# A hybrid decoder step on one core: all sample key products in the prompt search, value gathers behind them

## What is computed

```python
def trunk_layer(x, conv_past, ffn_past, attend, p):
    xn = rms_norm(x, g_attn)
    a_in, q, k, v, qi, ki, wi, ga, gb = split_in(xn @ w_in)
    glu = a_in[..., :D_CONV] * jax.nn.sigmoid(a_in[..., D_CONV:])
    h = layer_norm(causal_dwconv(glu_ext, conv_w, conv_b), ln_g, ln_b)
    y_a = jax.nn.silu(h) @ w_a_out
    q = rms_norm(q.reshape(b, t, N_HEADS, HEAD_DIM), q_g)
    k = rms_norm(k.reshape(b, t, N_HEADS, HEAD_DIM), k_g)
    o = attend(q, k, v, qi, ki, wi)
    x = x + (jax.nn.sigmoid(ga) * y_a + jax.nn.sigmoid(gb) * (o.reshape(b, t, D_ATTN) @ w_b_out)) @ w_o
...

def attend(q, k, v, qi, ki, wi):        # prompt and samples alike
    score = jnp.einsum('bqhl,bqh->bql', relu(qi . ki), wi) * IDX_SCALE   # future positions -inf
    idx = lax.top_k(score, n_keep)[1]
    logits = jnp.einsum('bqhd,bqkhd->bqhk', q, k_sel) * ATTN_SCALE + rel_bias[rel_bucket(q_pos - key_pos)]
    p = jax.nn.softmax(jnp.where(rel >= 0, logits, -inf))
    return jnp.einsum('bqhk,bqkhd->bqhd', p, v_sel)
```

## Time and profile before

| | |
|---|---|
| median of 3 runs | 1239.48 us (1238.52 to 1245.93) |
| the profiled execution | 1239.93 us |
| its span | 1238.1 us |
| busy: PE, DVE, ACT, POOL | 90%, 64%, 25%, 14% of the span |
| prompt search, steps 3 to 32 | 379 to 502 us |
| first head of the attention | 541.59 us |
| attention | 541.59 to 723.29 us |
| from yb to the end | 723.29 to 1238 us |
| mean granted clock of TensorE | 0.945 of 2.4 GHz |

### The profile page before, as it was taken

How to read it: one execution, slowest core, us unless ns; L and a number is a source line. 1 busy time by engine, 2 the same in 40 slices (tenths; PEclk the granted TensorE clock), 3 DMA queues, 4 the chain that set the end, 5 groups by cost and what they waited for, 6 DMA issues and landing times.

```text
span 1238.1 us, 16818 instructions
## 1 busy us (share of the span) xinstructions
PE 1111.8 (90%) x6732; PEld 894.5 (72%) x6732; DVE 788.8 (64%) x1576; ACT 311.1 (25%) x633; POOL 177.4 (14%) x187
## 2 busy tenths in 40 slices
PE   5999799999779998977574789999999999989996
PEld 3668688664557743435343368999999999989996
DVE  5299999688779889867571144586666565642211
ACT  2111233222201134422121223432223221241220
POOL 0011110000011123153673400000000000001011
PEclk9999899999889999986786899999999999999998
DMA  9110550013143455244765533123332323123230
GB/s 306 44 68 7 179 180 1 31 38 137 69 168 120 144 170 170 80 147 121 220 212 187 174 92 103 35 69 86 86 97 75 103 69 103 48 77 112 81 112 28
DMA packets 109607, 134.49 MB, mean 109 GB/s; under 512 B 8081, under 2 KB 76588, under 8 KB 108484
## 3 DMA queue, kind: packets, MB, share of 16 engines
q1 hardware_dynamic: 90997, 76.67, 20.4%
q0 software_dynamic: 13184, 45.42, 11.7%
q10 hardware_dynamic: 5349, 11.34, 2.6%
HBM read 127.89 MB, written 5.51 MB: 108 GB/s over the span
## 4 chain that ended last, share of the span: by engine, by line
PE 70%; DVE 18%; ACT 4%; issue 3%; another core or an unknown queue 3%; DMA 0%; ACTq 0%; DVEq 0%
PE G L1265 12%; PE G L1267 12%; PE G L1266 12%; PE G L990 8%; PE G L755 6%; PE G L775 6%; DVE hT L1482 4%; PE TB L1112 2%; ACT late L2240 2%; DVE junk L1576 2%; PE UB L1208 1%; DVE ksel L1792 1%; PE G L1081 1%; DVE scoreT L1544 1%
## 5 line engine op out<-in xcount | busy, mean ns | idle before, releaser
L1265 PE MATMUL G<-xnH,whi 128*128 128x274 f32 x704 | 205.2, 291 | 1.1 <-DVE aext L1947 0.7
L1266 PE MATMUL G<-xnL,whi 128*128 128x274 f32 x704 | 203.5, 289 | 0.0
L1267 PE MATMUL G<-xnH,wlo 128*128 128x274 f32 x704 | 202.9, 288 | 0.0
L990 PE MATMUL G<-xnT,wring 128*128 128x280 f32 x512 | 141.4, 431 | 9.0 <-ACT sgb L2036 3.7
L1878 DVE TENSOR_TENSOR wlo<-wraw,whi 128x2048 fp32r<-128x2048 f32 (+1 forms) x38 | 76.4, 2011 | 91.1 <-ACT whi L2400 90.3
L1265 PEld LDWEIGHTS G<-xnH,whi 128*128 128x128 f32 x704 | 132.4, 188 | 1.7 <-issue 0.9
L1266 PEld LDWEIGHTS G<-xnL,whi 128*128 128x128 f32 x704 | 133.3, 189 | 0.0
L1267 PEld LDWEIGHTS G<-xnH,wlo 128*128 128x128 f32 x704 | 133.1, 189 | 0.0
L990 PEld LDWEIGHTS G<-xnT,wring 128*128 128x128 f32 x512 | 100.7, 203 | 39.9 <-issue 7.1
L2540 POOL DMA_INDIRECT ksel<-in_cache_k_dram,gather_row x64 | 70.5, 1102 | 351.6 <-DVE gather_row L1744 180.1
L1265 PE MATMUL G<-hfH,whi 128*128 128x274 f32 x352 | 102.6, 292 | 0.0
(11 more groups left out here) (417 smaller groups left out, 1970.5 us busy)
## 6 DMA issues: line engine op xcount, KB each, us to landing
wraw<-in_w_up_dram SPq DMA_DIRECT2D x44, 512.0 KB, 5.1
wring<-in_w_in_dram SPq DMA_DIRECT2D x8, 2048.0 KB
wraw<-in_w_down_dram SPq DMA_DIRECT2D x16, 704.0 KB, 4.4
qB<-scr_q SPq DMA_DIRECT2D x32, 256.0 KB
wring<-in_w_in_dram ACTq DMA_DIRECT2D x3, 2048.0 KB
wring<-in_w_o_dram SPq DMA_DIRECT2D x2, 2048.0 KB
toep<-scr_toep SPq DMA_DIRECT2D x1, 2432.0 KB, 15.4
wqi<-in_w_in_dram SPq DMA_DIRECT2D x2, 1024.0 KB, 9.8
```

Source lines behind the costliest of these rows:

```text
L990: last = pe.matmul(out[:, i, 0:b - a], w[:, j, c:c + P], x[:, j, a:b], start=(j == 0), stop=(j == depth - 1))
L1265: pe.matmul(out, w_hi, x_hi, start=start, stop=False)
L1266: pe.matmul(out, w_hi, x_lo, start=False, stop=False)
L1267: return pe.matmul(out, w_lo, x_hi, start=False, stop=stop)
```

## The change

The kernel after differs in where things stand in the engines' lists, and in the buffers of the values.

- DVE: all 32 key products stand in the search, one a step from step 3 and two in steps 16 and 24. Before, 14 stood there at every second step, 2 between the masks and 16 in the heads. The takes of ya are at steps 7 to 12. The norms of row tiles 1, 2, 3 stand in steps 27, 29, 31, `first_max` in step 28, and all three masks behind the search. Steps 9 and 10 are counted by ACT too.
- The norm of the last tile and the sample attention's pieces come at earlier heads.
- TensorE: the first `tokens` come ahead of head 8's transposes.
- ACT: the counts stand at other places of its list; from step 28 on, takes, copies, squares and the first tile's exponentials stand between them.
- POOL: all keys, then v's rows, then all values, into twelve buffers. SP's list is unchanged.

```diff
-    TOKENS_AT = {11: 0, 13: 1}
+    TOKENS_AT = {9: 0, 11: 1}
...
-    AT_BIAS, AT_LOGITS = {12: 0, 29: 1}, {13: 0, 29: 1}
-    AT_MAX, AT_WEIGHTS, AT_PROBS, AT_OUT = {14: 0, 30: 1}, {15: 0, 31: 1}, {16: 0, 32: 1}, {28: 0, 39: 1}
-    AT_QUADS = {17: 0, 19: 1, 22: 2, 27: 3, 33: 4, 35: 5, 37: 6, 39: 7}
-    FIRST_KEYS = 14
-    AT_KEYS = {11: 16, 13: 17, 14: 18, 15: 19, 16: 20, 17: 21, 18: 22, **{a: a + 3 for a in range(20, 29)}}
-    AT_LAST_ROW, AT_LAST_MASK = 11, 19
-    FIRST_TAKE = 9
+    AT_BIAS, AT_LOGITS = {11: 0, 22: 1}, {12: 0, 23: 1}
+    AT_MAX, AT_WEIGHTS, AT_PROBS, AT_OUT = {13: 0, 24: 1}, {14: 0, 25: 1}, {15: 0, 26: 1}, {21: 0, 35: 1}
+    AT_QUADS = {16: 0, 17: 1, 19: 2, 20: 3, 27: 4, 29: 5, 31: 6, 33: 7}
+    AT_LAST_ROW, AT_LAST_MASK = 10, 19
+    FIRST_KEY, KEY_TWICE = 3, (16, 24)
+    TAKE_STEPS = (7, 8, 9, 9, 10, 11, 12, 12)
+    NORM_AT = {27: 1, 29: 2, 31: 3}
+    FIRST_MAX_AT = 28
+    VALUE_COUNTS = (15, 16, 18, 19, 21)
...
+    def keys_by(i):
+        return max(0, i + 1 - FIRST_KEY + sum(i >= at for at in KEY_TWICE))
+    def taken_by(i):
+        return sum(at <= i for at in TAKE_STEPS)
+    VALUE_HOMES = [0, 1, 2, 3, 4, 5, 9, 10, 11, 6, 7, 8] + [3, 4, 5, 0, 1, 2, 9, 10, 11, 6, 7, 8] + [0, 1, 2, 9, 10, 11, 6, 7]
...
-    COUNTED_STEPS = [i for i in range(COMPARE + 1) if i < 3 or i >= 11]
+    COUNTED_STEPS = [i for i in range(COMPARE + 1) if i < 3 or i >= 9]
...
         logits_pair(N_HEADS)
+        tokens(TOKENS_AT[N_HEADS + 1])
         for a in range(N_HEADS, ATTEND):
...
             prompt_units(4, compared_late)
-            if i % 2 == 0 and i // 2 - 2 in range(FIRST_KEYS):
-                key_product(i // 2 - 2)
-            if i - FIRST_TAKE in range(KM):
-                branch_take(i - FIRST_TAKE)
-        prompt_mask(1)
-        pair_norm(1)
-        dve.wait_ge(S["toep_loaded"], 16)
-        first_max()
-        pair_norm(2)
-        prompt_mask(2)
-        pair_norm(3)
-        key_product(FIRST_KEYS)
-        prompt_mask(3)
-        key_product(FIRST_KEYS + 1)
+            for t in range(keys_by(i - 1), keys_by(i)):
+                key_product(t)
+            for n in range(taken_by(i - 1), taken_by(i)):
+                branch_take(n)
+            if i in NORM_AT:
+                pair_norm(NORM_AT[i])
+            if i == FIRST_MAX_AT:
+                dve.wait_ge(S["toep_loaded"], 16)
+                first_max()
+        for r in range(1, NT - 1):
+            prompt_mask(r)
...
-            if a in AT_KEYS:
-                key_product(AT_KEYS[a])
...
         pair_out(1)
+        take_pair(1)
+        counts(29)
         first_exp()
-        take_pair(1)
         pair_in("q", 3)
+        counts(30)
         pair_out(2)
         pair_in("k", 3)
         pair_squares(3)
         first_probs()
+        counts(32)
         take_pair(2)
         pair_in("q", 4)
+        counts(COMPARE + 1)
         pair_in("k", 4)
...
-            if i >= 9:
-                pool.wait_ge(S["pv_used"], i - 8)
+            if i >= 12:
+                pool.wait_ge(S["pv_used"], value_before(i) + 1)
             gather(v_rows, value_buffer(i)[0], value_buffer(i)[1], value_token(i))
-        for i in range(17):
+        for i in range(NS):
             keys(i)
...
-        for i in range(17, 19):
-            keys(i)
-        ready(pool, ("k", NT - 1))
-        for i in range(6):
-            values(i)
-        for i in range(19, 21):
-            keys(i)
-        for i in range(21, NS):
-            values(i - 15)
-            keys(i)
-        for i in range(NS - 15, NS):
+        for i in range(NS):
             values(i)
```

More of the change, by code:

```diff
@@ L522, in value_token, with value_before @@
         return 16 * (i // 16) + 4 * (i % 4) + i % 16 // 4
+    def keys_by(i):
[3 more added lines that the diff above has]
+    VALUE_HOMES = [0, 1, 2, 3, 4, 5, 9, 10, 11, 6, 7, 8] + [3, 4, 5, 0, 1, 2, 9, 10, 11, 6, 7, 8] + [0, 1, 2, 9, 10, 11, 6, 7]
     def value_buffer(i):
-        at, turn = i % 9, i // 9
-        if 3 <= at < 6 and turn >= 2:
-            return ksel[at - 3], s_ksel[at - 3], 32 * (len(range(at - 3, NS, 3)) + turn - 1)
+        at = VALUE_HOMES[i]
+        turn = VALUE_HOMES[:i].count(at)
+        if at >= 9:
+            return ksel[at - 9], s_ksel[at - 9], 32 * (len(range(at - 9, NS, 3)) + turn + 1)
         return vsel[at], s_vsel[at], 32 * (turn + 1)
+    def value_before(i):
+        return max(j for j in range(i) if VALUE_HOMES[j] == VALUE_HOMES[i])
     def tiles(r):
@@ L1166, in bias @@
             pe.wait_ge(S["hotk_ready"], 2 * g + 2)
+            pe.wait_ge(S["nat_done"], 2 * NT)
             if g == 0:
@@ L1852, in _ @@
                 at_max(a + 1)
+            if a == N_HEADS - 1:
+                pair_factor(NT - 1)
             if a == N_HEADS:
-                pair_factor(NT - 1)
-            if a == N_HEADS + 1:
                 pair_scale(NT - 1)
@@ L2268, in _ @@
         gate("gb", 3)
-        gate("gb", 4)
-        counts(6)
-        gate("gb", 5)
-        counts(8)
-        gate("gb", 6)
-        counts(10)
-        gate("gb", 7)
+        for n in range(4, KM):
+            gate("gb", n)
         next_weights("v")
         for r in range(NT):
-            counts(20 + 2 * r)
+            counts(VALUE_COUNTS[r])
             take_value(r)
@@ L2347, in first_probs @@
             step(act.activation(pT8[1][:, :, :], x[:, 6:8, :], ACT.Copy), free, free=True)
-        counts(30)
+        counts(23)
         pair_in("q", 1)
-        counts(32)
+        counts(24)
         pair_in("q", 2)
-        counts(COMPARE + 1)
+        counts(26)
         pair_in("k", 1)
         pair_squares(1)
+        counts(27)
         pair_in("k", 2)
+        counts(28)
         pair_squares(2)
         pair_out(1)
+        take_pair(1)
+        counts(29)
         first_exp()
-        take_pair(1)
         pair_in("q", 3)
+        counts(30)
         pair_out(2)
```

4 lines of the change are left out of this document (2 added, 2 removed).

## The result

The changed kernel takes 1277.56 us (median of 4 runs, 1276.03 to 1278.97), the kernel before beside it 1240.14: a ratio of 1.0293, interval 1.0257 to 1.0329. It is slower by 37 us; I had forecast 12, with a range that ended at 1274. The profiled execution of after took 1276.9, its span is 1275.1, 37.0 longer than before's.

What follows compares the result with a forecast made beforehand. It took DVE to bound the search and TensorE's late results to slow the attention: 582.7 to the first head + 131.7 + 21 = 735.4 against 723.29, +12.1, so 1252 us (own range 1244 to 1260; overall 1226 to 1274).

Steps and rivals of the forecast that it cites:

- Search, +41.1: Start to first head: 16 more key products and smaller terms add 41.1 us, moving the first head from 541.59 to 582.7.
- The wait for ya: Search: takes start at step 7 instead of 9, so the first waits longer for ya's product, +0.9 us.
- ACT's counts: Search, steps 28 to 30: DVE waits while ACT does other work between its counts, +7.0 us, bounds 0 and +11.
- the two waits behind the search: Second norm's wait of 2.94 and first head's of 1.54 get steps in front of them, -4.5 us.
- Lateness of before, 42: Attention of the kernel before: TensorE's late results make 42 of its 181.7 us, leaving 139.7 without them.
- 4.7 us of TensorE's own work: Attention before: two groups of value products inside the long unknown-queue pieces, subtracted from their 40.8 us.
- Lateness after, 52 x 0.40 = 21: Attention after: 52 value gathers under the heads at 0.40 us of lateness each, 21 us, bounds 0 and 33.
- Rival 3: Attention: long stalls stay in full as quads stand closer, 33 us rather than 21, clock gives nothing back: 1268, chance 0.15.
- The rest of the attention, -8: Attention without lateness: first eight heads -1, tail -3, clock -4, so 139.7 becomes 131.7 us.
- a clock of 0.80 from 0.76: Attention: TensorE is busier in a shorter stretch, its clock rises, 6 us of which 4 on the path: -4.
- Behind yb, 0: Stretch after yb's start: same work at the same clock of 0.99, unchanged at 515 us.

Runs made afterwards that it cites:

- e8_norms_behind: The changed kernel with row norms and first maximum behind the search again and ACT's counts ahead of its other work: 1270.9 us, kernel before 1247.3.
- e7_before_plain: Kernel before, keys and values from the first value gather on fetched by plain DMAs of consecutive rows (not the picked ones): 1199.7 us against 1247.3.
- e2_plain_values: The changed kernel with each value buffer fetched by two plain DMAs of consecutive rows (not the picked ones): 1238.6 us, kernel before 1247.7.
- e14: Kernel before with a 64 x 64 memset that POOL waits for behind each indirect gather from the first value gather on: 1235.5 us against 1246.4.
- e3: The changed kernel with half of the value gathers, one per token, read by both halves of a quad's matmuls: 1242.8 us, kernel before 1247.7.
- e4: The changed kernel with value quads two heads apart, second group's scores 3 heads later, all 64 value gathers kept: 1262.5 us, kernel before 1247.7.
- e12: The changed kernel with one of each token's two value gathers as a plain DMA of consecutive rows: 1236.4 us, kernel before 1243.7.
- e13: Kernel before with a plain DMA of 256 bytes behind each indirect gather from the first value gather on: 1251.8 us against 1246.4.
- e15: The changed kernel with a plain DMA of 256 bytes behind each value gather, nothing left out: 1256.7 us, kernel before 1246.4.
- e5: The changed kernel, but POOL waits until a token's values have landed before issuing the next token's: 1295.1 us, kernel before 1247.3.
- e6: Kernel before, but from its first value gather on POOL waits for each token's gathers to land before the next: 1339.6 us against 1247.3.
- e11_search_alone: Kernel before with all 32 key products in the search and the changed POOL list; heads, norms, counts and buffers as before: 1258.9 us against 1243.7.
- e18: Kernel before with a 64 x 64 memset that POOL waits for behind each value gather only, keys as they were: 1237.2 us against 1244.4.

## Why the prediction was wrong

Point by point, by its own steps.

- **Search, +41.1: right**, +42.0 measured. The wait for ya was 3.6 (+0.9 as said). ACT's counts cost 13.0 against 4.5 in the same stretch before, +8.5 rather than +7.0, and the two waits behind the search vanished. Counted against the same products with the norms behind the search, interleaving them was a loss of some 3 us (e8_norms_behind), not a gain.
- **Lateness of before, 42: right in size**, 42.6 by e7_before_plain, with some luck in the parts. I took 4.7 us of TensorE's own work off the pieces of the unknown queue, and it is 14.5. In its place stand work that goes faster in the plain form (120.4 us of TensorE's in before, 111.6 in e7) and waits for transfers that e7's chain has and before's hasn't.
- **Lateness after, 52 x 0.40 = 21: wrong**, 37.6 by e2_plain_values. This is the step that failed: it priced late results by the gather and by idle time alone, and beside it the sum let the clock rise. Of the 37.6 us, 25.0 are TensorE idle in late pieces and 12.0 are its own work at a clock of 0.70 instead of the 0.78 that it has without them. The idle part was mis-sized by little: 25.0 us over the 54 gathers that are issued under the heads is 0.46 for one, and by the same count before has 0.40 (36 us over 91, its idle time in the unknown pieces and the issue pieces over 1.3 us, without the 1.98 at 542.31 that e14 has too). But the price isn't fixed: it was nothing for the first 14 gathers under the heads and 0.73 for the 24 from 635.41 on; with half the gathers more than half went (e3), with the quads apart 7 us of idle time went (e4), and with a plain DMA between the gathers (e12, e13, e15) or a landing waited for (e5, e6) no copy of ACT's came late. 16.0 of the 24.9 us by which the sum was short lie here. Rival 3 had the right sign and size (33, and a clock that gives back nothing); that the closer quads play a part is borne out by e4.
- **The rest of the attention, -8: half**, -3.3 (135.8 against 139.1). The first eight heads did not get shorter but longer, 40.6 us against 37.1 in the two plain kernels. I had taken a clock of 0.80 from 0.76; the measured one is 0.70 over the attention, and 0.54 in the first eight heads where before had 0.62. In the 20 us ahead of the first head TensorE was busy 9.3 at 0.74; in before it was busy 19.9 at 1.00. The longer search alone doesn't do this: e8_norms_behind and e11_search_alone also come in with 19.9 of 20 us at 1.00, and both have 0.62. What differs in after is that the norms, the first maximum and the ACT work for them stand in the search; e8 puts them back. In e8 the first eight heads take 39.6 us with a late piece of 1.9 in them, so of the 3.5 us between 40.6 and 37.1 this accounts for 1 to 3; the rest, and what the changed tables add, is open.
- **Behind yb, 0: +3.3** (518.1 against 514.8). Variants of the kernel before on other chips have 514.9 to 518.7 there, so I can't say that it is the change.

41.1 - 8 - 21 = 12.1 became 42.0 - 3.3 - 5.0 + 3.3 = 37.0.

The Trainium skill (SBUF — State Buffer, "Who interferes with whom") says of access to SBUF that PE never waits on anyone and that DMA never contends with a compute engine. For the plain DMAs of 256 KB the traces agree: in e2 and e7 no copy of ACT's comes more than 1 us behind TensorE. For the indirect ones I had applied the rule to the time at which TensorE's results arrive, and there 14 us lie between the recorded end of transposes and what they release (655.28, 670.27). Whether TensorE itself stands still or only its signals are held can't be told from these runs, so they don't show that the rule is wrong.

What stays open: why after's 18 gathers from 570.57 to 595.1, with no quad in them, delay no copy of ACT's, while the streams that quads meet do; whether it is the plain DMA or the longer time between gathers (1.83 us against 1.39) that helps where the memset didn't; and by what path POOL's work holds TensorE's results.

## What to carry to other kernels

A stall that the profile gives to "another core or an unknown queue" on one core is a measurable thing: put the suspected transfer in another form with the same bytes, and the difference is its price, which here was 37.6 and 42.6 us of some 1240. Before reading a piece of the chain as idle time, look how much of it the engine worked: here more than a third of it. The price of a stall can also be more than its length: without the late results the same matmuls were granted 0.78 instead of 0.70, which was 12.0 of the 37.6 us. And work moved into a stretch that one engine bounds costs its full length there (here 2.4 us for each of 16 products).

## What was not expected of the hardware

- TensorE's results reach ACT up to 14 us late while POOL issues indirect DMAs every 1.25 us without a break. With a plain DMA of 256 bytes behind each (1.83 us apart) none came over 1 us late.
- A memset of 0.17 us and its wait behind each (1.39 us apart) takes most of it away (37.9 to 6.9 us in before, 28.1 to 4.6 in after), but not reliably: in e18 12.6 us came late in a stretch with a memset behind every gather.
- An indirect gather of 256 KB lands about 3.5 us after POOL has issued it, so waiting for each token makes 5.6 us of 2.5.
